# Layer attention taken map by map, its scores made of two fp32r products

## The reference, cut to what matters

```python
# four "diff" heads of two maps each (m = 0, 1), keys of 64
s = einsum('bhmqd,bhmkd->bhmqk', qb, k) * scale        # masked by chunks of 64
p = softmax(s)
a = p[:, :, 0] - lam * p[:, :, 1]
do = rmsnorm(einsum('bhqk,bhkd->bhqd', a, v), subln_gain) * (1 - lam_init) * silu(dg)
# eight "fox" heads, keys of 64
s = einsum('bhqd,bhkd->bhqk', qb, k) * scale + cq[..., None] - cum_logf[:, :, None, :]
fo = einsum('bhqk,bhkd->bhqd', softmax(causal(s)), v) * silu(fg)
h = h + concatenate([do, fo]) @ w_out
```

## Time and profile before

| | |
|---|---|
| median of 3 runs | 1856.77 us (1856.63 to 1857.36) |
| the profiled execution | 1856.04 us, its span 1854.2 us |
| PE busy | 1825.4 us (98%), granted clock 1.00 |
| DVE / ACT / POOL busy | 62% / 42% / 26% |
| layer 0 attention, first score to first `wout` matmul | 203.86 to 321.15 us: 117.29 us |
| layer 1 attention | 558.00 to 667.05 us: 109.05 us |

### The profile page before, as it was taken

The page is one execution under the profiler, slowest core; times in us unless marked ns, Lnnn a source line. Parts: engine busy times, 40 slices in busy tenths (PEclk is TensorE's granted clock), DMA queues, the critical chain, the costliest instruction groups (busy, mean ns, idle before and its releaser), DMA issues.

```text
span 1854.2 us, 29748 instructions
## 1 busy us (share of the span) xinstructions
PE 1825.4 (98%) x12068; PEld 1635.7 (88%) x12068; DVE 1156.7 (62%) x1671; ACT 769.8 (42%) x1394; POOL 481.8 (26%) x352
## 2 busy tenths in 40 slices
PE   9999999999999999999999999999999999999999
PEld 8999888979988887999988877989877879999887
DVE  7542465555416657999985555646666589999531
ACT  4122455321235644444433323446565554444331
POOL 5433211354341123000034433320143410000343
PEclk9999999999999999999999999999999999999999
DMA  4222100223220012333322323210003213323223
GB/s 166 97 85 85 42 2 23 74 91 98 82 91 13 24 35 91 114 126 103 103 75 91 102 98 126 82 35 1 1 1 114 92 63 120 126 92 103 73 98 102
DMA packets 41048, 145.49 MB, mean 78 GB/s; under 512 B 5072, under 2 KB 5328, under 8 KB 40784
## 3 DMA queue, kind: packets, MB, share of 16 engines
q1 hardware_dynamic: 40912, 143.59, 23.0%
HBM read 140.40 MB, written 2.10 MB: 77 GB/s over the span
## 4 chain that ended last, share of the span: by engine, by line
PE 89%; DVE 6%; ACT 3%; issue 1%; DMA 1%; POOL 0%; SPq 0%; DVEq 0%; ACTq 0%
PE ps L472 23%; PE ps L473 23%; PE ps L474 23%; PE ps L1070 6%; PE ps L1101 5%; PE ps L1086 2%; PE ps L2678 1%; PE ps L2664 1%; DMA raw<-wstream 1%; PE ps L2647 1%; DVE xl L564 1%; PE ps L1280 1%; PE ps L2417 1%; ACT wh L448 1%; DVE nm L1147 0%
## 5 line engine op out<-in xcount | busy, mean ns | idle before, releaser
L456 POOL TENSOR_TENSOR wl<-raw,wh 128x1024 fp32r<-128x1024 f32 (+1 forms) x168 | 406.7, 2421 | 1024.6 <-ACT wh L448 1024.5
L448 ACT ACTIVATE wh<-raw 128x1024 fp32r<-128x1024 f32 (+1 forms) x178 | 188.9, 1061 | 601.9 <-PE ps L474 535.9
L472 PE MATMUL ps<-xh,wh 128*128 128x264 f32 (+3 forms) x1144 | 385.1, 337 | 4.7 <-ACT wh L448 2.5
L473 PE MATMUL ps<-xl,wh 128*128 128x264 f32 (+3 forms) x1144 | 381.4, 333 | 0.0
L474 PE MATMUL ps<-xh,wl 128*128 128x264 f32 (+3 forms) x1144 | 380.8, 333 | 0.0
L474 PE MATMUL ps<-XSh,wl 128*128 128x256 f32 (+1 forms) x864 | 283.8, 328 | 0.0
L472 PE MATMUL ps<-XSh,wh 128*128 128x256 f32 (+1 forms) x864 | 283.4, 328 | 0.3 <-DVE wl L1753 0.3
L473 PE MATMUL ps<-XSl,wh 128*128 128x256 f32 (+1 forms) x864 | 283.5, 328 | 0.0
L472 PEld LDWEIGHTS ps<-xh,wh 128*128 128x128 f32 x1144 | 215.5, 188 | 31.5 <-issue 9.0
L473 PEld LDWEIGHTS ps<-xl,wh 128*128 128x128 f32 x1144 | 215.6, 188 | 22.6 <-issue 1.2
L474 PEld LDWEIGHTS ps<-xh,wl 128*128 128x128 f32 x1144 | 215.7, 189 | 21.8
(11 more groups left out here) (428 smaller groups left out, 3523.9 us busy)
## 6 DMA issues: line engine op xcount, KB each, us to landing
raw<-wstream SPq DMA_DIRECT2D x176, 512.0 KB, 3.3
rawx<-wpairs SPq DMA_DIRECT2D x44, 512.0 KB, 3.6
raw<-wpairs SPq DMA_DIRECT2D x24, 512.0 KB, 3.5
raw<-wstream SPq DMA_DIRECT2D x10, 528.0 KB, 3.4
h<-xT SPq DMA_DIRECT2D x4, 528.0 KB, 5.9
out<-h SPq DMA_DIRECT2D x8, 256.0 KB, 4.4
xs<-wpairs SPq DMA_DIRECT2D x2, 512.0 KB, 4.4
HF<-wpairs SPq DMA_DIRECT2D x2, 512.0 KB, 5.5
```

The lines of the kernel that those rows point to most:

```text
L448: e.activation(wh[p % 2][:, 0:n], raw[c % 2][:, 0:n], ACT.Copy).then_inc(*w_hi(p))
L456: e.tensor_tensor(wl[p % 2][:, 0:n], raw[c % 2][:, 0:n], wh[p % 2][:, 0:n].bitcast(F32), ALU.subtract).then_inc(*w_lo(p))
L472: e.matmul(o, w_h, x_h, start=start, stop=False)
L473: e.matmul(o, w_h, x_l, start=False, stop=False)
```

## The change

- **Scores.** `query_high_act` and `query_low_dve` put the high part of a query half into its 64 rows of QA or QB (now fp32r) and the low part into the other 64 rows, instead of zeros. For each map or head a key tile is copied by two DMAs to both halves of a raw tile (`key_copies`, on SP), then split by ACT (`key_high_act`) and DVE (`key_low_dve`). A score is then Q against the high key part plus Q against the low one, two fp32r matmuls. There are 16 such keys in a layer, two ahead of the attention, the others at the steps of `KEY_STEP`. They live in KX, in wh, wl and in spent query tiles. The memsets of QA and QB go; QZ (256 columns) keeps the 16 meta queries with zeros.
- **Order.** The units go map by map: for a diff head c the four blocks i, each with its two maps, interleaved with the fox heads. `banks_of` now chooses a unit's banks and `ahead` together. A PSUM out bank holds the four query blocks of one head. The ends run for a head (`c`) over all 512 tokens.
- **Ends.** A diff end first copies the sums out of PSUM (ACT, `"copy"`), which frees the bank; the square and the scale then read the copy. The gate is one instruction of 512 columns instead of four of 128.
- **Values.** The second half of the last value projection runs tile by tile: two before step 0, one each in steps 1, 2, 3. All copies of turned probabilities but the quads' move to ACT (`third=1000`).
- **Meta quads.** POOL writes the meta values of each quad anew (`quad_values_pool`).
- **Output projection.** Tiles 0 and 1 are begun over the k whose heads are done, and finished over the rest; the low part of weight tile 2 is taken by DVE.

Core of the diff:

```diff
-            for j in range(2):
-                e.tensor_tensor(QA[64 * j:64 * j + 64, 2 * c + j, c0:c0 + n], u[64 * j:64 * j + 64],
-                                v[64 * j:64 * j + 64], ALU.add).then_inc(*roped(*key, "add", j))
+                e.tensor_tensor(u, u, v, ALU.add).then_inc(*roped(*key, "add", 1))
...
+        def query_high_act(e, on, key):
+            src, to = query_parts(key)
+            on.wait_ge(*(roped[key + ("add", 1)] if key[0] == "dq" else v_out[key]))
+            for j, b in enumerate((0, 64)):
+                r = e.activation(to[b:b + 64, j, :], src[b:b + 64], ACT.Copy)
...
+        def query_low_dve(e, on, key):
...
+            for j, b in enumerate((0, 64)):
+                r = e.tensor_tensor(to[64 - b:128 - b, j, :], src[b:b + 64], to[b:b + 64, j, :].bitcast(F32), ALU.subtract)
...
+        KEY_STEP = dict(zip(KEYS[2:], (5, 6, 7, 9, 14, 17, 19, 21, 28, 31, 33, 37, 44, 47)))
...
+        def key_copies(e, on, l, kind, c, q):
...
+            on.wait_ge(*(roped["dk", l, 2 + i, "sin"] if i < 2 else v_lo["fq", l, 3] if i == 2 else
+                         v_lo[("key", l) + KEYS[i - 2 - (i < 5)]]))
+            for b in (0, 64):
+                e.dma_start(key_raw_at((kind, c, q))[b:b + 64], src).then_inc(d_key[n % 4], 16)
...
+        def key_high_act(e, on, l, kind, c, q):
...
+            e.activation(high, key_raw_at((kind, c, q)), ACT.Copy).then_inc(*a_out("key", l, kind, c, q))
...
+        def key_low_dve(e, on, l, kind, c, q):
...
+            e.tensor_tensor(low, key_raw_at((kind, c, q)), high.bitcast(F32), ALU.subtract).then_inc(
...
+        VALUES_PE, VALUES_ACT, VALUES_DVE = {-1: 2, 1: 1, 2: 1, 3: 1}, {2: (1,), 4: (3,)}, {1: (0,), 3: (2,), 5: (4,)}
...
-            if l:
-                on.wait_ge(*tile["wout", 0, 7])
-                for q, Q in enumerate(Q_of[l]):
-                    e.memset(Q[:, :, :], 0.0).then_inc(*p_one("clear", l, q))
...
+                if x.lows:
+                    on.wait_ge(*v_lo[x.lows])
...
-                    terms.append((Q[:, m, c0:c0 + 128], K[:, m // 2, a:b], a, b, True, not fox and not masked))
+                    terms.append((Q[:, m, c0:c0 + 128], khigh[:, a:b], a, b, True, False))
+                    terms.append((Q[:, m, c0:c0 + 128], klow[:, a:b], a, b, False, not fox and not masked))
...
+            pairs = maps[:4] + heads[:2] + [x for pair_ in zip(maps[4:], heads[2:-2]) for x in pair_] + heads[-2:]
...
+            for c, ks in ((0, (0, 1, 2, 4, 5, 6)), (1, (0, 1, 2))):
...
+                product(c, ks, True)
+                if c == 0:
                     end_pe(e, on, plans[l], *plans[l].held)
+            product(0, (3, 7), False).then_inc(*tile("wout", l, 0))
+            product(1, (3, 4, 5, 6, 7), False).then_inc(*tile("wout", l, 1))
```

More of the change, by code:

```diff
@@ new lines, in key_home, with last_score @@
+        def key_home(l, kind, c, q):
+            if (kind, c) in (("diff", 0), ("diff", 2), ("fox", 3)):
+                return KX[:, q, 0, :], KX[:, q, 1, :]
+            if kind == "diff" and c == 3:
+                return Q_of[l][q][:, 0, :], Q_of[l][q][:, 1, :]
+            t = wh[q] if kind == "diff" else wl[PART["wout", l, q] % 2]
+            return t[:, 0:L], t[:, L:2 * L]
+        def last_score(l, kind, c, q):
+            plan = plans[l]
+            return score[plan.name, max(u for u, x in enumerate(plan.units) if x.key == (kind, c, q))]
@@ L801, in proj_act @@
             for j, (kind, c) in enumerate(FEATS):
+                key = (kind, l, c)
                 if l == 0 and j == 10:
@@ L1003, in __init__ @@
                 for u, x in enumerate(units):
-                    after = int(bool(x.quad) and not x.pair)
+                    after = int(bool(x.quad))
                     if x.job:
@@ L1088, in attention_pe @@
                 begin_pe(e, on, plan, s)
+                if values and s in VALUES_PE:
+                    next(values)
                 for u in plan.flips.get(s - 1, []):
@@ L1514, in layer_plan @@
[L1514 to L1519 removed]
+            used, at = {0: -4, 1: -4, 2: -4, 3: 0}, [-1]
@@ L1532, in layer_plan @@
                 u = len(units)
-                hh = m if fox else m // 2
-                four, place_ = divmod(m if fox else m // 2, 4)
-                if place_ == 0 and (fox or m == 0):
-                    quads[kind] = Quad(kind, 2 * i + four if fox else i, out_at[key])
-                units.append(Unit(
-                    terms=terms, n=n, o0=112, banks=banks_of(u, wide, range(3 if beside_meta else 4)),
-                    ready=[(v_one, ("ncl", l))], total=(rs[:, 2 * fox + i % 2, m:m + 1], was), group=key,
+                hh = m if fox else c
@@ new lines, in layer_plan @@
+                col = 256 * q + 64 * i if fox else 128 * i
+                tiles = [x[2] for two_ in heads for x in two_ if x[1] == c and x[3] == q] if fox else list(range(4))
+                place_ = tiles.index(i)
+                if place_ == 0 and (fox or q == 0):
+                    quads[kind] = Quad(kind, m if fox else c, out_at[key])
+                units.append(Unit(
+                    terms=terms, n=n, o0=112, **banks_of(u, wide, [y[2] == 3 for y in queue[u:] + maps[3]].index(True)),
+                    ready=[(v_one, ("ncl", l))], group=key,
+                    total=(rs[:, 2 * fox + c % 2, 4 * q + i:4 * q + i + 1] if fox else
+                           rs[:, c % 2, 2 * i + q:2 * i + q + 1], was),
+                    key=(kind, c, q), lows=("key", l, kind, c, q),
@@ L1541, in layer_plan @@
                     blocks=[(M + 128 * j, M + 128 * j + 128) for j in range(i + 1)],
                     value=lambda j, rows_, V=V, hh=hh, hd=hd: V[0:rows_, j + 1, hd * hh:hd * hh + hd],
-                    quad=(quads[kind], place_) if fox or m % 2 else None,
-                    cols=(hd * hh, hd * hh + hd), ahead=1 if wide else 2 if beside_meta else 3,
-                    job=3 if fox or m % 2 else 0, pair=not fox and m % 2 == 1, third=1000 if fox else 4,
-                    first=m == (0 if fox else 1), last=m == 7, out_bank=out_at[key]))
@@ L1547, in layer_plan @@
-                if m == 7:
+                    quad=(quads[kind], place_) if fox or q else None, tile=i,
+                    cols=(col, col + hd),
+                    job=3 if fox or q else 0, pair=not fox and q == 1, third=1000,
+                    first=place_ == 0 and q == (0 if fox else 1), last=place_ == 3 and q == 1, out_bank=out_at[key]))
+                if place_ == 3 and q:
                     last_unit[key] = ("quad", u)
             if l == 0:
-                for kind, step in (("diff", 1), ("fox", 22)):
+                for kind, step in (("diff", 12), ("fox", 28)):
```

367 lines of the change are left out of this document (250 added, 117 removed).

## The result

The changed kernel takes **1859.86 us** (median; 1858.07 to 1870.18) against 1856.8 before: a ratio of 1.0018 (95% interval 1.0011 to 1.0025), within what counts as no change here. The forecast was 1833 (1820 to 1850): it is wrong by 27 us and the time lies outside its range. The profiled execution has a span of 1856.8 us, 2.6 above the one before (1854.2).

| stage | before | after | difference | forecast |
|---|---|---|---|---|
| up to the first score | 203.86 | 202.80 | -1.06 | -1.2 |
| attention, layer 0 | 117.29 | 122.14 | **+4.85** | -10 |
| output tiles, layer 0 | 55.44 | 53.10 | -2.34 | -2.5 |
| start of layer 1 | 13.59 | 12.18 | -1.41 | -1.2 |
| projections, layer 1 | 167.82 | 167.82 | 0 | 0 |

A forecast was written before the change was run, and what follows sets the result against it. PE, busy for 98% of the span, was taken as the bound. From profiled 1856.04 us, - 24.3 (scores) + 8 (attention gives back) - 5.0 (output tiles) - 2.4 (memsets) gave 1832.3, median 1833; range 1820 to 1850.

The forecast's parts named there:

- Scores: Layer attentions: two fp32r matmuls replace one float32 matmul per score; 12.2 us saved a layer, 24.3 in both (bounds 19 and 27).
- What the attention gives back: Both attentions: idle PE time added by work on ACT and DVE and by the new order; 8 us (bounds 0 and 16).
- The body that was walked: Layer 1 attention, steps 22 to 30: 1.3 us idle in nine steps, carried to 6.4 in 44 steps; 10.4 idle a layer.
- The ramp: Attention from first score to step 11: 19.8 us for 15.9 of work, 4 idle, mainly at the first fox unit.
- The early stop of the sums: Attention heads' ends: the copy frees bank 6 before the next head's first product, so nothing waits; cost nothing.
- Output tiles: First output tile of each layer: begun over finished heads, its matmuls cost less time; 2.5 + 2.45 = 5.0 us saved.
- Memsets: Layers' starts: PE waits of 1.21 and 1.26 us behind POOL's clearing of QA and QB both go; 2.4 us saved.
- Projections, SP, keys made ahead of the attention: Projections: query splits and key copies moved there fit beside PE's tiles; taken as nothing (bound 1 us a layer).
- the wide units: Rival, attention scores: wide units wait for maximum and exp to free their banks, 48 us in place of 8; 1873 us, chance 9%.
- The projections: Rival, projections: new DVE subtracts fall among POOL's weight splits and delay the next split, 18 us; 1851 us, chance 10%.
- Nothing is given back: Rival, attentions: value tiles fill the ramp, so the 8 us are not lost; 1825 us, 1822 at the upper price, chance 15%.
- two products cost what one did: Rival, attention scores: fp32r runs no faster on these operands, so 24.3 us is not saved; 1857 us, chance 3%.

The follow-up runs named there:

- e3: Kernel before with Q and K rounded to fp32r and two fp32r products per score, block order kept, low parts left out: 1842.82 us, second attention 98.82.
- e4: Changed kernel with the products undone, each score one float32 product with the key's high part: 1873.69 us, second attention 121.91.
- e5: Changed kernel without any work on keys, scores taken straight from rounded KA and KB, new order kept: 1848.39 us, second attention 106.72.
- e2: Changed kernel without the key's low part: DVE subtracts one column, second score product reads the high part again: 1855.05 us, second attention 110.53.
- e16: Changed kernel without the copy of the diff sums; square and scaling read the bank as in the kernel before: 1857.25 us, second attention 111.29.
- e17: Changed kernel with every step of the ends of diff heads 0 to 2 one step later, copy kept: 1856.00 us, second attention 111.53.
- e6: Changed kernel with ten spare 512-column products in each of three PE waits (unit 8 in both layers, unit 17 in layer 0): 1856.22 us.

## Why the prediction was wrong, step by step

- **Scores** (24.3 less): as work, right: 25.4. In time, in layer 1's attention, 10.2 of 12.7 us in block order (e3) and 8.9 in the new one (e4 against the changed kernel): a shorter list meets waits even where the order is good. The forecast let the whole of it count.
- **What the attention gives back** (8 more): here it failed. The two attentions, with 25.4 us less work, came out 8.85 us longer, so they gave back 34 us. In layer 1 it is 16.7: 2.5 that the shorter list loses in the old order already, 7.9 for the order and 6.3 for the key parts (e3, e5 and e2, and the changed kernel). Less 12.7 us, the forecast's own work of 108.9 and 104.4 us is 96.2 and 91.7, so PE loses 25.9 us (some 5 of them to the clock) and 21.3 us (some 2), where the walk gave 10.4. The body that was walked, units 22 to 30, was walked right (1.3; by distances of starts PE loses 1.4 there). But its 0.14 a step was carried over to 44 steps, and it is the quietest part: it holds no end of a diff head. The eight units behind it lose 3.0, units 46 to 53 lose 3.6 (the page's idle times for the same, above, are 0.56, 1.90, 0.43 and 2.55). The ramp, forecast at 4 us idle until step 11, lost 4.6.
- **The early stop of the sums** (nothing): the argument looked at the bank, and PE's list of waits indeed has none for the copy that frees it. It did not ask what stands behind copy and square in ACT's queue: an exp, and behind that a bank (e16, e17).
- **Loads**: ACT was forecast at 77 us a stretch and DVE at 75 to 81; they are 74 to 76 and 78 to 84. Loads of three quarters of the planned stretch were read as room; with ACT and PE waiting for each other in turn they were not. e2 prices DVE's share (2.5 us a layer), e5 and e2 the key parts (6.3 with it).
- **The clock**: there was no term for it. The earlier trace rows shows 1.00 throughout, and the forecast took that as given; the waits that it foresaw itself, 2.5 us at the first fox unit of each layer, stand ahead of two of the four stretches at half clock, and with these and a third wait filled all four are gone (e6). About 6.6 us.
- **Output tiles** (5.0 less): 4.75. **Memsets** (2.4 less): 2.5. **Projections, SP, keys made ahead of the attention** (nothing): 167.82 us before and after. (The term's five times add up to 12.36, not 12.45; nothing hangs on it.)

Of the rivals, the wide units had the right engine pair (exp and bank) and the wrong place: the waits follow the heads' ends, and the time is nearer to no change than to 1873. The projections did not stretch. "Nothing is given back" is refuted by 17 us a layer, and "two products cost what one did" by the spacing, though its time, 1857, came closest.

Of the order's 7.9 us a layer, only a part is explained. e17 shows what the waits at units 34 and 50 are made of, but its second attention is only 1.5 us shorter (111.53 for 113.04), at a lower clock (0.97 for 0.98). The wait for DVE's scaled sums is read from the trace below, and no run takes it away alone. The others (the longest is 1.3 us, where transposes wait for a copy of ACT) were not taken apart.

## What to carry to other kernels

When a piece of a loop is walked, take the piece in which most things fall together, not a quiet one, and carry its loss only to pieces of its kind. An operation put on an engine with spare time must be read in that engine's order: what stands behind it, and who waits for that. And when a faster PE begins to wait, price the clock too: here stretches at half clock came behind waits of 2.3 to 2.5 us, and work that nobody needs, put into three of them, was worth 3.6 us.

## What the runs showed of the hardware that was not expected

- The granted clock fell from 1.00 to 0.50 (1.2 GHz) for 3.40 us behind stretches that held a wait of 2.50 and of 2.26 us (PE busy for 12.49 of 15.00 us, and for 11.34 of 13.60). Matmuls took 1.8 times as long in it: two of 400 columns 0.81 us, where two at full clock take 0.45 (608.32 to 608.77 above):

```profile
236.35 1.01 PE L1179 MATMUL ps<-wl,QB 128*128 128x400 f32 x2
237.16 0.54 PE L1179 MATMUL ps<-NCh,maskR 128*128 128x400 f32 x1
```

- A DVE operation on two operands of SBUF stood still while POOL split an output weight tile: four columns took 1.91 us (the layer's other three such operations some 0.16), a head's low part 1.73 us (0.68 in the earlier trace rows). The four columns are a step in the end of diff head 2; the scaling behind them came some 1.75 us later for it, and PE's transposes waited for that, 1.26 us in each layer (2.5 in the list of PE's waits above). The forecast has no term for it. DVE, POOL, then PE:

```profile
640.78 1.91 DVE L1492 TENSOR_TENSOR small<-small 128x4 f32<-128x4 f32 x1 [0.16 <-ACT small L1450]
646.30 1.73 DVE L1563 TENSOR_TENSOR xl<-xb,xh 128x512 fp32r<-128x512 f32 x1
```

```profile
640.30 2.37 POOL L460 TENSOR_TENSOR wl<-raw,wh 128x1024 fp32r<-128x1024 f32 x1
645.12 2.37 POOL L460 TENSOR_TENSOR wl<-raw,wh 128x1024 fp32r<-128x1024 f32 x1
```

```profile
643.56 0.63 PE L1415 MATMUL ps<-identR,tmpn 128*128 128x128 f32 x4 [1.26 <-DVE tmpn L1495]
```

The Trainium skill's rule that the forecast weighed for the projections (SBUF — State Buffer, Who interferes with whom) holds here to the end of POOL's instruction; in the projections, where PE's tiles are longer than the delay, it cost nothing.
